# Recurrences stage of a two-block sequence model: rows of the next head issued one step earlier, and three memory tiles placed at other points of the TensorE queue

## The chip, the cores and the metric

The kernel runs on one core of one Trainium2 chip. The metric is device time in microseconds (us). The kernel before takes 3651.59 us, the median of three runs that lie between 3649.14 and 3654.63 us.

## The reference, cut to what matters

The program computes two blocks one after the other for 512 positions of width 1024. The first block projects its input and sends the parts through four sequence mixers, each of four heads. Two of them are decayed attentions in the form that concerns us:

```
# mLSTM, per head: a causal matrix of weights times scores, then a weighted sum of v and of ones
scores = (q . k) / 8 * exp(min(row[t] + col[s], 0)) * causal(s <= t)
num, den = scores @ v, sum(scores)
# SSD (Mamba-2), per head: the same with scores shared by all heads and another row and column
y = ((c . b) * exp(min(row[t] + col[s], 0)) * causal) @ x + d_skip * x
y = rms_norm(y * silu(z)) * gain
```

The second block attends in each of its two layers to a memory of 256 rows. Its keys and values depend on inputs alone: `mkv = mem @ w_mem_kv`, 8 tiles of 128 columns in each layer, 16 tiles in all. They can be computed anywhere ahead of the second block, and the kernel computes them in the stage called recurrences, between the matmuls of the mixers.

## The kernel before, in words

Each stage of the program is a block with one instruction list for each engine. An engine executes its list in order; semaphores carry the dependences; at the end of a stage all engines meet at a barrier (`stage`, line 165). The whole stage that concerns us is the function `recurrences` (line 593), with the class `MemoryTiles` (line 519) for the memory.

The scores of a head are laid out with the source position s on partitions. So a head is four steps j = 0..3: in step j the 128 source positions of block j meet all target positions from block j on, which makes tiles of 128 partitions by 512, 384, 256 and 128 elements. The four heads make 16 steps n = 4h + j, the list `steps`. The mLSTM loop comes first, then the SSD loop; names with `m_` and `s_` tell them apart. A step goes through these engines:

- TensorE: `m_rows(h)` (line 728, matmul L733), once a head, spreads the row of the head over all 128 partitions into PSUM bank 6. It waits until the last exponent of the head before has been read from that bank. In the SSD loop this is `s_rows(h)` (line 755, matmul L760).
- VectorE: `m_exponents(n)` (L1010), or `s_exponents(n)` (L1029), adds the column and clips at zero. The exponents of step n + 1 are in VectorE's list ahead of the weights of step n.
- ScalarE: `m_exps(n)` (L894), `s_exps(n)` (L899): the exponential.
- TensorE, mLSTM alone: `m_score(n)` (L742), q against k, in banks 4 and 5 by turns. The SSD scores were made before and lie in SBUF as `same`.
- VectorE: the causal mask on the diagonal block (L1016, L1035), then the product of scores and decay (L1021, L1041), in double buffers `matt` and `satt`.
- TensorE: `m_sums(n)` (L752 for the values, L753 for the ones, each 64 columns wide), `s_sums(n)` (L766).

TensorE's list in the mLSTM loop is, for each n: `m_score(n + 1)`; if n is the last step of a head, `m_rows` of the next head; `m_sums(n)`; then smaller things that belong to the norms of the other mixers. In the SSD loop it is: if n is the last step of a head, `s_rows` of the next; `s_sums(n)`; matmuls of the norms; and half a memory tile.

A memory tile t takes 24 matmuls of 256 columns. Its weights come from HBM (`sync_load`), ScalarE makes their high part (`scalar_high`, L572), VectorE the low part (`vector_low`, L590), TensorE multiplies (`tensor`, L555, L556 and L561, 12 matmuls in the first half and 4 + 8 in the second), ScalarE copies the result out of PSUM (`scalar_take`, L578), and SyncE stores it (`sync_store`, L540). Two buffers of each kind go round. The first matmul of a tile waits until the result of the tile before has been copied out. Tile 7 stands in the mLSTM loop behind the sums of steps 2 and 3, tiles 8 to 15 in the SSD loop, half a tile behind each of the 16 steps. Tile 15 is the last.

Two of the buffers for the low parts are `kv_low0` and `kv_low1`. The second lies under the first two tiles of `y`, where the SSD output `ys` goes. So VectorE waits, before it writes `ys` (L1184), until all 16 tiles have been multiplied (line 1182).

Behind the SSD loop comes the norm of the SSD output, one step at a time: VectorE adds the skip term (L1184, two instructions) and gates (L1186); ScalarE squares (L981); TensorE sums over the channels (L675); ScalarE takes the root (L984), in front of which it loads a table; VectorE inverts (L1188); TensorE spreads the inverse (L874); VectorE scales (L1192). With this the stage ends, once the stores have landed too (`sync_end`, line 542).

Of the kernel before, what the change touches and what calls it, by code (L numbers as in the profile page):

```python
# [14 lines left out]
P = 128  # L15
# [577 lines left out]
def recurrences(K, U, gate_up, g, bonus, y, memory):  # L593
# [9 lines left out]
    with ExitStack() as ctx:  # L603
# [8 lines left out]
        vt = K.sb(ctx, "vt", [P, NT, 256])  # L612
        kt = K.sb(ctx, "kt", [P, NT, P])
        b = K.sb(ctx, "b", [P, S])
        e = K.sb(ctx, "e", [P, 2, S])
        qd = K.sb(ctx, "qd", [P, S])
        ki = K.sb(ctx, "ki", [P, S])
# [20 lines left out]
                 "m_abs", "em_spread", "m_max", "m_timed", "m_gated", "m_mean", "m_centred", "m_squared", "m_var", "m_root", "m_inverse", "m_spread",  # L638
                 "s_row", "s_exponent", "s_decayed", "s_masked", "s_weighted", "s_summed",
                 "s_gated", "s_squared", "s_var", "s_root", "s_inverse", "s_spread"]  # L640
        kv_bank = lambda t: B[:, (1 if t < MEM_TILES or t == 9 or t == 11 else 2 if t in (13, 15) else 7), 0:MEM]
        with stage(nc, *names, *MEMORY_SEMS) as (block, *sems):
            memory.signals(sems[len(names):])
            (own, a_own, picked, logit, r_mean, turned, v_taken, a_ready, g_abs, g_exp, g_log, rows_ready,
# [25 lines left out]
            def _(pe):  # L670
# [140 lines left out]
                for n in range(LAST):  # L811
                    if n + 1 < LAST:
                        m_score(n + 1)
                    if n % NT == NT - 1 and n + 1 < LAST:
                        m_rows(n // NT + 1)
                    if n == 2 * NT:
                        pe.wait_ge(memory.taken, MEM_TILES)
                    m_sums(n)
                    if n in (2, 3):
                        memory.tensor(pe, MEM_TILES - 1, n % 2, kv_bank(MEM_TILES - 1))  # L820
                    if n == 1:
                        for t in range(2):
                            pe.wait_ge(l_squared, t + 1)
                            mm = quarter_sums(B[:, 7, t * P:(t + 1) * P], heads, t, True, True)
                        mm.then_inc(l_var, 1)
                    if n == 5:
                        pe.wait_ge(l_inverse, 1)
                        head_spread(B[:, 7, :], 0).then_inc(l_spread, 1)
                    if n == 8:
                        pe.wait_ge(l_scaled, 1)  # L830
                        head_spread(B[:, 7, :], 1).then_inc(l_spread, 1)
# [5 lines left out]
                    mm = nc.tensor.matmul(B[o, h // 2, :], K.c("pick", H, h)[:, 0:64], rows[:, 4, :], start=True, stop=True)  # L837
                mm.then_inc(em_spread, 1)
                for n in range(LAST):
                    if n % NT == NT - 1 and n + 1 < LAST:  # L840
                        s_rows(n // NT + 1)
                    s_sums(n)
                    if n in (5, 6):
                        t = n - 5
                        pe.wait_ge(m_gated, t + 1)
                        nc.tensor.matmul(B[:, 2 + t, :], K.c("mean64"), ym[:, t, :], start=True, stop=True).then_inc(m_mean, 1)
                    if n == 9:
                        for t in range(2):
                            pe.wait_ge(m_squared, t + 1)
                            mm = quarter_sums(B[:, 0, t * P:(t + 1) * P], heads, t, True, True)  # L850
                        mm.then_inc(m_var, 1)
                    t = MEM_TILES + n // 2
                    if n == 0:
                        pe.wait_ge(l_scaled, 2)
                    if n == 2:
                        pe.wait_ge(m_max, 1)
                    if n == 10:
                        pe.wait_ge(m_centred, 2)
                    memory.tensor(pe, t, n % 2, kv_bank(t))
                    if n == 12:  # L860
                        pe.wait_ge(m_inverse, 1)
                        head_spread(B[:, 1, :], 0).then_inc(m_spread, 1)
                        head_spread(B[:, 0, :], 1).then_inc(m_spread, 1)
                pe.wait_ge(s_exponent, LAST)
                for t in range(2):
                    pe.wait_ge(s_squared, t + 1)
                    mm = quarter_sums(B[:, 6, 0:P], K.c("mean256")[:, 0:32], t, t == 0, t == 1)
                mm.then_inc(s_var, 1)
                pe.wait_ge(s_inverse, 1)
                pe.wait_ge(l_scaled, 2)  # L870
                pe.wait_ge(memory.taken, memory.count)
                for c in range(NT):
                    row = K.c("ident")[:, 32 * c:32 * c + 1].to_broadcast([P, P])
                    mm = nc.tensor.matmul(B[:, 7, L[c]], row, root[:, 0, :], start=True, stop=True)  # L874
# [3 lines left out]
            def _(act):  # L878
# [68 lines left out]
                    nc.scalar.activation(sq[:, t, :], yl[:, t, :], ACT.Square).then_inc(l_squared, 1)  # L947
                for n in range(LAST):
                    m_exps(n)
                    if n == 5:  # L950
                        memory.scalar_take(act, MEM_TILES - 1, kv_bank(MEM_TILES - 1))
                        memory.scalar_high(act, MEM_TILES + 1)
                    if n == 3:
                        act.wait_ge(l_var, 1)
                        act.wait_ge(r_scaled, 2)
                        nc.scalar.activation(root[:, :, :], B[:, 7, 0:2 * P].rearrange("p (a b) -> p a b", a=2), ACT.Sqrt,
                                             bias=K.c("eps", P, 0, 1)).then_inc(l_root, 1)
                act.wait_ge(m_summed, LAST)
                nc.scalar.activation(dn[:, :, :], B[:, 0:2, :], ACT.Abs).then_inc(m_abs, 1)
                for n in range(LAST):  # L960
                    s_exps(n)
                    if n >= 3 and n % 2:
                        t = MEM_TILES + (n - 3) // 2
                        memory.scalar_take(act, t, kv_bank(t))
                        if t + 2 < memory.count:
                            memory.scalar_high(act, t + 2)
                    if n == 8:
                        for t in range(2):
                            act.wait_ge(m_centred, t + 1)
                            act.wait_ge(l_var, 1)  # L970
                            nc.scalar.activation(sq[:, t, :], ym[:, t, :], ACT.Square).then_inc(m_squared, 1)
                    if n == 10:
                        act.wait_ge(m_var, 1)
                        act.wait_ge(l_scaled, 2)
                        nc.scalar.activation(root[:, :, :], B[:, 0, 0:2 * P].rearrange("p (a b) -> p a b", a=2), ACT.Sqrt,
                                             bias=K.c("eps", P, 0, 1)).then_inc(m_root, 1)
                memory.scalar_take(act, memory.count - 1, kv_bank(memory.count - 1))
                act.wait_ge(s_gated, 1)
                act.wait_ge(m_var, 1)
                for t in range(2):  # L980
                    nc.scalar.activation(sq[:, t, :], ys[:, t, :], ACT.Square).then_inc(s_squared, 1)  # L981
                act.wait_ge(s_var, 1)
                act.wait_ge(m_spread, 2)
                nc.scalar.activation(root[:, 0, :], B[:, 6, 0:P], ACT.Sqrt, bias=K.c("eps", P, 0, 1)).then_inc(s_root, 1)  # L984

            @block.vector
            def _(dve):
# [191 lines left out]
                        step.go(nc.vector.scalar_tensor_tensor(ym[:, t, :], ym[:, t, :], K.col("mlstm_norm_g", t), B[:, bank, :],  # L1179
                                                               ALU.mult, ALU.mult))  # L1180
                dve.wait_ge(s_summed, LAST)
                dve.wait_ge(memory.product, memory.count)
                for t in range(2):
                    step.go(nc.vector.scalar_tensor_tensor(ys[:, t, :], xc[:, t, :], K.col("ssd_d", t), B[:, 4 + t, :], ALU.mult, ALU.add))  # L1184
                step.all()
# [1556 lines left out]
def first_block(K, a, x, outer):  # L2742

    nc = K.nc
    with ExitStack() as ctx:
        gates = K.sb(ctx, "gates", [P, NT, EXPERTS])
        c1 = ctx.enter_context(ExitStack())
        with ExitStack() as held:
            kv_low1 = K.sb(held, "kv_low1", [P, D], F32R)
        y = K.sb(c1, "y", [P, DT, S])  # L2750
        with ExitStack() as c2:
            with ExitStack() as held:
                K.sb(held, "kept_tiles", [P, R_, S])
                kv_raw0 = K.sb(held, "kv_raw0", [P, D])
                kv_high0 = K.sb(held, "kv_high0", [P, D], F32R)
                kv_low0 = K.sb(held, "kv_low0", [P, D], F32R)
                kv_raw1 = K.sb(held, "kv_raw1", [P, D])
                kv_high1 = K.sb(held, "kv_high1", [P, D], F32R)
                kv_out = K.sb(held, "kv_out", [P, 2, MEM])
            U = K.sb(c2, "U", [P, U_TILES, S])  # L2760
            K.first = K.sb(c2, "first", [P, FIRST_W])
            gate_up = K.sb(c2, "gate_up", [P, P])
            lora = K.sb(c2, "lora", [P, 256])
            g = K.sb(c2, "g", [P, 2, S])
            bonus = K.sb(c2, "bonus", [P, 2, S])
            opening(K, a, x, y, U, lora, gate_up, g, bonus)
            memory = MemoryTiles(K, a, y[:, 4:8, :].rearrange("p t (a m) -> p (t a) m", m=MEM), [kv_raw0, kv_raw1], [kv_high0, kv_high1],
                                 [kv_low0, kv_low1], kv_out)
            recurrences(K, U, gate_up, g, bonus, y, memory)
        with lasting(nc, "kept") as (kept,):  # L2770
            arrival(K, a, x, y, gates, kept, lambda t: K.col("ln1_g", t), lambda t: K.col("ln1_b", t))
            K.mu = K.ps(outer, "x_mu", [P, S])
            mixture(K, a, x, gates, kept, lambda t: K.col("ln2_g", t), lambda t: K.col("ln2_b", t))
        c1.close()
# [1404 lines left out]
```

## Time and profile before

| | |
|---|---|
| three runs, median | 3651.59 us (3649.14 to 3654.63) |
| profiled execution | 3646.04 us, its span 3644.1 us |
| mean granted clock of TensorE | 0.959 of full speed |
| recurrences, from the first mLSTM row to the last scaling | about 390.3 to 518.4 us of the span |

The span is the time from the first instruction to the last in one profiled execution. Times in the trace count from the start of this span. PE is TensorE's matmuls, PEld its weight loads, DVE VectorE, ACT ScalarE, SP SyncE. The granted clock of TensorE is given as a share: 1.00 is 2.4 GHz, 0.50 is 1.2 GHz.

### The profile page before, as it was taken

The page shows a single profiled execution, that of the slowest core. Times are in us where ns is not written, and L with a number is a line of the kernel's source. Part 1 is how long each engine was busy: PE and PEld are TensorE (multiplying, and loading weights), DVE is VectorE, ACT ScalarE, POOL GpSimd, SP SyncE. Part 2 cuts the span into 40 slices and gives each one's busy share as a digit, 9 for nine tenths or more (in the row PEclk, how much of TensorE's full clock was granted, in tenths as well). Part 3 has the DMA queues.
Part 4 walks back from the last instruction along what each step waited for, and adds up shares of the span by engine and source line. Part 5 has one row for each costly group of instructions (what it writes and reads, how often), then busy time and mean ns, then how long its engine had stood idle before and what let it go on. Part 6 is the DMA issues. An engine that isn't in the chain of part 4 may idle for free. (4 is left out here: it accounts for less than half of the span.)

```text
span 3644.1 us, 44870 instructions
## 1 busy us (share of the span) xinstructions
PE 3421.1 (94%) x16696; PEld 2724.1 (75%) x16696; DVE 2505.8 (69%) x2841; ACT 1909.5 (52%) x2146; POOL 209.3 (6%) x202
## 2 busy tenths in 40 slices
PE   8998877999999999999989897999999999799998
PEld 7886455888888888888758775678887877578886
DVE  6654455999999999999657757466526776646542
ACT  4223233887778777777545445254316435434422
POOL 0000000111111111211000000000000000000000
PEclk9988888999999999999989998999999999899999
DMA  4111135999999999999511110133322111023331
GB/s 152 41 30 42 46 109 212 352 367 367 365 369 364 371 368 364 367 366 373 189 55 59 58 57 18 48 104 98 101 79 79 55 53 53 22 72 104 97 100 63
DMA packets 118800, 600.24 MB, mean 165 GB/s; under 512 B 20722, under 2 KB 24194, under 8 KB 68130
## 3 DMA queue, kind: packets, MB, share of 16 engines
q1 hardware_dynamic: 105346, 580.93, 43.8%
q0 software_dynamic: 13312, 17.35, 1.9%
q8 instruction: 98, 1.61, 0.2%
q14 instruction: 44, 0.36, 0.0%
HBM read 586.06 MB, written 28.90 MB: 169 GB/s over the span
## 5 line engine op out<-in xcount | busy, mean ns | idle before, releaser
L2326 DVE TENSOR_TENSOR wl<-raw,wh 128x2048 fp32r<-128x2048 f32 x384 | 873.0, 2287 | 55.5 <-ACT wh L2256 55.5
L2256 ACT ACTIVATE wh<-raw 128x2048 fp32r<-128x2048 f32 x384 | 735.7, 1916 | 192.4 <-PE pu L2201 146.7
L2199 PE MATMUL pu<-wh,Xh 128*128 128x512 f32 x1024 | 410.5, 401 | 0.0
L2200 PE MATMUL pu<-wl,Xh 128*128 128x512 f32 x1024 | 400.4, 391 | 0.0
L2201 PE MATMUL pu<-wh,Xl 128*128 128x512 f32 x1024 | 400.2, 391 | 0.0
L4019 ACT ACTIVATE w_high<-w_raw 128x1024 fp32r<-128x1024 f32 (+1 forms) x120 | 137.0, 1145 | 334.5 <-PE acc L3993 172.0
L4052 DVE TENSOR_TENSOR w_low<-w_raw,w_high 128x1024 fp32r<-128x1024 f32 (+1 forms) x120 | 159.6, 1331 | 199.1 <-PE ps L3951 107.6
L3975 PE MATMUL ps<-x_high,w_high 128*128 128x512 f32 x656 | 255.2, 389 | 0.0
L3976 PE MATMUL ps<-x_low,w_high 128*128 128x512 f32 x656 | 255.2, 389 | 0.0
L2199 PEld LDWEIGHTS pu<-wh,Xh 128*128 128x128 f32 x1024 | 193.0, 188 | 45.9 <-issue 8.1
L2201 PEld LDWEIGHTS pu<-wh,Xl 128*128 128x128 f32 x1024 | 192.9, 188 | 42.5
L2956 PE MATMUL acc<-x_high,w_high 128*128 128x512 f32 x528 | 221.0, 419 | 1.5 <-ACT hq L3287 1.5
L2200 PEld LDWEIGHTS pu<-wl,Xh 128*128 128x128 f32 x1024 | 193.1, 189 | 37.3
L2957 PE MATMUL acc<-x_low,w_high 128*128 128x512 f32 x528 | 209.5, 397 | 0.0
L2199 PE MATMUL pd<-wh,hh 128*128 128x512 f32 x512 | 208.5, 407 | 0.2 <-DVE hl L2340 0.2
L2200 PE MATMUL pd<-wl,hh 128*128 128x512 f32 x512 | 200.1, 391 | 0.0
L2201 PE MATMUL pd<-wh,hl 128*128 128x512 f32 x512 | 200.0, 391 | 0.0
L3538 DVE TENSOR_TENSOR w_low<-w_raw,w_high 128x1024 fp32r<-128x1024 f32 (+1 forms) x104 | 118.3, 1141 | 90.4 <-PE acc L2962 64.0
L3951 PE MATMUL ps<-x_high,w_low 128*128 128x512 f32 x704 | 173.2, 389 | 0.0
L3951 PEld LDWEIGHTS ps<-x_high,w_low 128*128 128x128 f32 x704 | 132.1, 188 | 27.5
L3988 PE MATMUL acc<-h_high,w_high 128*128 128x512 f32 x352 | 143.2, 407 | 1.5 <-DVE h_low L4086 1.5
L3975 PEld LDWEIGHTS ps<-x_high,w_high 128*128 128x128 f32 x656 | 123.1, 188 | 25.6
(710 smaller groups left out, 6852.2 us busy)
## 6 DMA issues: line engine op xcount, KB each, us to landing
raw<-in_exp_w SPq DMA_DIRECT2D x384, 1024.0 KB, 7.7
w_raw<-in_w_in SPq DMA_DIRECT2D x100, 512.0 KB, 3.4
w_raw<-in_w_up SPq DMA_DIRECT2D x88, 512.0 KB, 3.8
w_raw<-in_w_down SPq DMA_DIRECT2D x32, 704.0 KB, 4.0
w_raw<-in_w_out SPq DMA_DIRECT2D x32, 384.0 KB, 3.1
kv_raw<-in_w_mem_kv SPq DMA_DIRECT2D x16, 512.0 KB, 3.7
x<-in_x SPq DMA_DIRECT2D x4, 1024.0 KB, 7.4
w_raw<-in_w_out SPq DMA_DIRECT2D x8, 512.0 KB, 4.3
```

The lines of the kernel that those rows point to most:

```text
L2199: nc.tensor.matmul(o, lh[:, k, :], wh[:, m % PARTS, c], start=(m >= 8 and kh == 0 and kk == 0), stop=False)
L2200: nc.tensor.matmul(o, lh[:, k, :], wl[:, m % PARTS, c], start=False, stop=False)
L2201: mm = nc.tensor.matmul(o, ll[:, k, :], wh[:, m % PARTS, c], start=False, stop=end)
L2256: nc.scalar.activation(wh[:, m % PARTS, :], raw[:, m % RAW, :], ACT.Copy).then_inc(w_high, 1)
L2326: nc.vector.tensor_tensor(wl[:, m % PARTS, :], raw[:, m % RAW, :], wh[:, m % PARTS, :], ALU.subtract).then_inc(w_low, 1)
L2956: nc.tensor.matmul(o, wh[:, n % 3, c], high[:, k, :], start=(k == 0), stop=False)
L2957: nc.tensor.matmul(o, wh[:, n % 3, c], low[:, k, :], start=False, stop=False)
L3951: mm = nc.tensor.matmul(o, wl[:, u % 2, c], high[:, k, :], start=False, stop=(k == DT - 1))
L3975: nc.tensor.matmul(o, wh(u)[:, c], high[:, k, :], start=(k == 0), stop=False)
L3976: nc.tensor.matmul(o, wh(u)[:, c], low[:, k, :], start=False, stop=False)
L3988: nc.tensor.matmul(o, wh(u)[:, c], hh[:, f * PART + k, :], start=(f == 0 and k == 0), stop=False)
L4052: nc.vector.tensor_tensor(wl[:, u % 2, 0:width(u)], raw[:, u % 3, 0:width(u)], wh(u), ALU.subtract).then_inc(low_ready, 1)
```

## The change

In TensorE's list, `m_rows` and `s_rows` of the next head stand behind the sums of the head's third step (n % 4 == 2) instead of before the sums of its last step; in the mLSTM loop this puts the row ahead of `m_score` of the next head's first step, in the SSD loop ahead of the half memory tile of that step. Memory tile 7 moves in one piece in front of the sums of mLSTM step 0. Tiles 14 and 15 leave the SSD loop: tile 14 stands behind the loop in one piece, tile 15 behind the sums over squares (L675). On ScalarE the copies out of tiles 7, 14 and 15 move accordingly: behind the exponential of step 1, behind the squares, and behind the last root. The second low buffer lies under `e` instead of under `y`; `e` has been used up by then. With this the wait for all 16 tiles ahead of `ys` falls away. Tile 15 uses PSUM bank 3 instead of bank 2, and the last spread waits for 15 copies instead of 16.

```diff
@@ recurrences
         b = K.sb(ctx, "b", [P, S])
+        with ExitStack() as held:
+            memory.wl.append(K.sb(held, "kv_low1", [P, D], F32R))
         e = K.sb(ctx, "e", [P, 2, S])
@@
-        kv_bank = lambda t: B[:, (1 if t < MEM_TILES or t == 9 or t == 11 else 2 if t in (13, 15) else 7), 0:MEM]
+        kv_bank = lambda t: B[:, (1 if t < MEM_TILES or t == 9 or t == 11 else 2 if t == 13 else 3 if t == 15 else 7), 0:MEM]
@@ tensor, mLSTM loop
                     if n + 1 < LAST:
                         m_score(n + 1)
-                    if n % NT == NT - 1 and n + 1 < LAST:
-                        m_rows(n // NT + 1)
                     if n == 2 * NT:
                         pe.wait_ge(memory.taken, MEM_TILES)
+                    if n == 0:
+                        for half in (0, 1):
+                            memory.tensor(pe, MEM_TILES - 1, half, kv_bank(MEM_TILES - 1))
                     m_sums(n)
-                    if n in (2, 3):
-                        memory.tensor(pe, MEM_TILES - 1, n % 2, kv_bank(MEM_TILES - 1))
+                    if n % NT == NT - 2 and n + 2 < LAST:
+                        m_rows(n // NT + 1)
@@ tensor, SSD loop
-                    if n % NT == NT - 1 and n + 1 < LAST:
+                    s_sums(n)
+                    if n % NT == NT - 2 and n + 2 < LAST:
                         s_rows(n // NT + 1)
-                    s_sums(n)
@@
-                    memory.tensor(pe, t, n % 2, kv_bank(t))
+                    if n < 12:
+                        memory.tensor(pe, t, n % 2, kv_bank(t))
@@ tensor, behind the SSD loop
+                for half in (0, 1):
+                    memory.tensor(pe, memory.count - 2, half, kv_bank(memory.count - 2))
                 pe.wait_ge(s_exponent, LAST)
                 for t in range(2):
                     pe.wait_ge(s_squared, t + 1)
                     mm = quarter_sums(B[:, 6, 0:P], K.c("mean256")[:, 0:32], t, t == 0, t == 1)
                 mm.then_inc(s_var, 1)
+                for half in (0, 1):
+                    memory.tensor(pe, memory.count - 1, half, kv_bank(memory.count - 1))
                 pe.wait_ge(s_inverse, 1)
                 pe.wait_ge(l_scaled, 2)
-                pe.wait_ge(memory.taken, memory.count)
+                pe.wait_ge(memory.taken, memory.count - 1)
@@ scalar
-                    if n == 5:
+                    if n == 1:
                         memory.scalar_take(act, MEM_TILES - 1, kv_bank(MEM_TILES - 1))
                         memory.scalar_high(act, MEM_TILES + 1)
@@
-                    if n >= 3 and n % 2:
+                    if 3 <= n < 15 and n % 2:
@@
-                memory.scalar_take(act, memory.count - 1, kv_bank(memory.count - 1))
                 act.wait_ge(s_gated, 1)
                 act.wait_ge(m_var, 1)
                 for t in range(2):
                     nc.scalar.activation(sq[:, t, :], ys[:, t, :], ACT.Square).then_inc(s_squared, 1)
+                memory.scalar_take(act, memory.count - 2, kv_bank(memory.count - 2))
                 act.wait_ge(s_var, 1)
                 act.wait_ge(m_spread, 2)
                 nc.scalar.activation(root[:, 0, :], B[:, 6, 0:P], ACT.Sqrt, bias=K.c("eps", P, 0, 1)).then_inc(s_root, 1)
+                memory.scalar_take(act, memory.count - 1, kv_bank(memory.count - 1))
@@ vector
                 dve.wait_ge(s_summed, LAST)
-                dve.wait_ge(memory.product, memory.count)
@@ first_block: kv_low1 is no longer made under y, and MemoryTiles gets [kv_low0] alone
```

## Rows read from the trace of the kernel before

**Rows 1.** The page: span, and busy time of each engine with its share.

```profile
span 3644.1 us, 44870 instructions
PE 3421.1 (94%) x16696; PEld 2724.1 (75%) x16696; DVE 2505.8 (69%) x2841; ACT 1909.5 (52%) x2146; POOL 209.3 (6%) x202
```

**Rows 2.** Windows: stretch, length, busy time of each engine, granted clock, DMA.

```profile
core 0: us, PE busy (x) PEld busy (x) DVE busy (x) ACT busy (x) POOL busy (x), PEclk, DMA share, GB/s
390.30:449.40 59.10, 50.18 (x162) 20.82 (x161) 25.82 (x55) 16.50 (x28) 0.00 (x0) 0.83 0.08 23
449.40:508.30 58.90, 53.46 (x277) 35.16 (x276) 40.20 (x66) 20.71 (x36) 0.00 (x0) 0.88 0.19 61
493.50:504.70 11.20, 11.02 (x61) 8.47 (x62) 9.31 (x17) 3.11 (x7) 0.00 (x0) 0.85 0.04 14
```

**Rows 3.** TensorE in order of time: start, length, line, [idle before <- releaser].

```profile
389.24 1.12 PE L561 MATMUL B<-mem_parts,kv_low 128*128 128x256 f32 x8
...
391.95 1.77 PE L742 MATMUL B<-U 64*128 64x512 f32 x4 [0.54 <-ACT same L889]
397.13 1.94 PE L752 MATMUL B<-matt,mv 128*64 128x512 f32 x2 [3.41 <-DVE matt L1021]
...
405.06 0.39 PE L555 MATMUL B<-mem_parts,kv_high 128*128 128x256 f32 x1
...
406.69 1.12 PE L742 MATMUL B<-U 64*128 64x512 f32 x2
...
410.81 0.38 PE L555 MATMUL B<-mem_parts,kv_high 128*128 128x256 f32 x1
...
411.39 1.74 PE L561 MATMUL B<-mem_parts,kv_low 128*128 128x256 f32 x8
```

**Rows 4.** TensorE where the second mLSTM head ends.

```profile
422.88 1.12 PE L742 MATMUL B<-U 64*128 64x512 f32 x2
423.93 1.12 PE L733 MATMUL B<-rows,first 4*128 4x512 f32 x2
426.42 0.43 PE L752 MATMUL B<-matt,mv 128*64 128x128 f32 x2 [1.37 <-DVE matt L1021]
```

**Rows 5.** VectorE at the same place.

```profile
425.09 0.75 DVE L1010 TENSOR_SCALAR mdec<-B,gate_cols 128x512 f32<-128x512 f32 x1 [4.43 <-PE B L733]
```

**Rows 6.** TensorE at the second and ahead of the third turn of SSD heads.

```profile
478.40 1.12 PE L760 MATMUL B<-rows,first 4*128 4x512 f32 x2
480.89 0.43 PE L766 MATMUL B<-satt,xt 128*64 128x128 f32 x2 [1.37 <-DVE satt L1041]
...
489.59 0.36 PE L555 MATMUL B<-mem_parts,kv_high 128*128 128x256 f32 x1 [0.39 <-ACT kv_out L578]
```

**Rows 7.** Windows of one granted clock each.

```profile
394.50:401.40 6.90, 4.27 (x6) 1.25 (x6) 2.78 (x7) 3.84 (x6) 0.00 (x0) 0.51 0.00 0
411.60:418.40 6.80, 6.80 (x15) 2.64 (x14) 3.50 (x7) 1.94 (x4) 0.00 (x0) 0.50 0.31 96
428.70:432.10 3.40, 3.40 (x4) 0.60 (x4) 2.18 (x6) 0.72 (x2) 0.00 (x0) 0.50 0.00 0
449.30:452.50 3.20, 3.09 (x11) 0.76 (x10) 1.80 (x4) 2.07 (x3) 0.00 (x0) 1.00 0.00 0
418.40:428.60 10.20, 8.14 (x30) 3.70 (x31) 4.89 (x10) 1.15 (x2) 0.00 (x0) 1.00 0.01 2
```

**Rows 8.** VectorE behind the SSD loop.

```profile
508.31 1.41 DVE L1184 SCALAR_TENSOR_TENSOR y<-U,cols,B 128x512 f32<-128x512 f32 x2 [3.60 <-PE B L561]
...
516.99 1.41 DVE L1192 SCALAR_TENSOR_TENSOR y<-y,cols,B 128x512 f32<-128x512 f32 x2 [2.17 <-PE B L874]
```

**Rows 9.** ScalarE behind the SSD loop.

```profile
512.18 1.28 ACT L984 ACT_TABLE_LOAD   x1
```

**Rows 10.** TensorE's last spread.

```profile
514.88 2.07 PE L874 MATMUL B<-root,const 128*128 128x128 f32 x8 [2.01 <-DVE root L1188]
```

**Rows 11.** The stores of the memory tiles (L540), from issue to landing.

```profile
DMA to landing us min/median/max: 1.9/2.2/3.8
```

More of the change, by code:

```diff
@@ L2747, in first_block @@
         c1 = ctx.enter_context(ExitStack())
-        with ExitStack() as held:
-            kv_low1 = K.sb(held, "kv_low1", [P, D], F32R)
         y = K.sb(c1, "y", [P, DT, S])
@@ L2767, in first_block @@
             memory = MemoryTiles(K, a, y[:, 4:8, :].rearrange("p t (a m) -> p (t a) m", m=MEM), [kv_raw0, kv_raw1], [kv_high0, kv_high1],
-                                 [kv_low0, kv_low1], kv_out)
+                                 [kv_low0], kv_out)
             recurrences(K, U, gate_up, g, bonus, y, memory)
```

## The prediction

> **What bounds the kernel now.** I read the page first: TensorE is busy 94% of the span [rows 1], so time goes where TensorE waits, or where it works at half clock. The page's chain of waits holds nothing of use here (it follows only the last microseconds), so I went to windows. The two loops take 59.1 and 58.9 us, with TensorE busy 50.2 and 53.5, at a mean clock of 0.83 and 0.88; VectorE is busy 25.8 and 40.2 [rows 2]. So TensorE sets the pace in both, with two losses: gaps, and stretches at half clock.
>
> The gaps are in TensorE's order of time. It idles 3.41 us ahead of the first sums [rows 3] and 1.37 us at a turn of heads [rows 4]. The rows show why: score of the next head (from 422.88), row (from 423.93), and only then can VectorE begin, at 425.09 after 4.43 us of waiting [rows 5]; it makes the next head's exponents first and then the weights that TensorE's next sums need, at 426.42. The same 1.37 us stands at all six turns; one of SSD is shown [rows 6].
>
> The clock: behind several of these gaps TensorE runs at 0.50 for a while [rows 7]. Of 128x512 and smaller matmuls everything then takes twice as long: the eight matmuls of a tile's low part took 1.12 us at full clock and 1.74 us where the clock fell just after their start [rows 3].
>
> **The change, part by part.** Stages meet at barriers, so what the stage loses the program loses.
>
> (a) Tile 7 into the first gap. Before, its first half stands between 405.06 and 406.69 (1.63 us), its second between 410.81 and about 413.05 (the eight low matmuls from 411.39 last 1.74; 2.24 us) [rows 3]. Together 3.9 us leave TensorE's path. At the new place 24 matmuls at 1.12 / 8 = 0.14 us, overlapping to about 0.12, take 2.9 us, and the gap from 393.7 to 397.13 is 3.4 us: hidden. If the clock falls ahead of it the tile takes 5.2 us and 1.8 show. Queued behind it are only `m_sums(0)` and what follows. On ScalarE, its copy and the high part of tile 9 (0.38 + 1.05 us) now stand ahead of the exponential of step 2; VectorE waits there for the score of step 2 anyway, so nothing. Gain 3.9, bounds 2.1 and 3.9.
>
> (b) Three mLSTM rows. The row no longer stands behind the 512-column score, which takes 1.05 us start to start [rows 4]. VectorE gets it 1.05 us earlier, and the score fills 1.05 of the 1.37 us gap. Gain 3 x 1.05 = 3.2; the remaining 0.3 us gap stays. Below: the score now comes 1.1 us later than the row, but VectorE needs it only after 2.9 us of exponents, mask and weights, so no loss.
>
> (c) Three SSD rows. Between row and last sums now lies half a memory tile (12 matmuls, 1.4 us or more), longer than VectorE's 1.37 [rows 6]. So the gap goes whole, 3 x 1.37 = 4.1. At the third turn the row also fills a wait of 0.39 for the copy out of tile 12 [rows 6]. Together 4.5. In the first SSD head VectorE is tied up in two reciprocals and comes free just as the row lands, so its turn could lose 0.5: bounds 3.6 and 4.5.
>
> (d) The end of the SSD loop. Tiles 14 and 15 leave. Before, from the last row's turn (about 493.6) to `ys` (508.31) pass 14.7 us, TensorE-bound. Without the two tiles VectorE sets the pace: 9.31 us busy in 493.5 to 504.7 [rows 2], then the last sums, 0.4 us: 9.8. Its work there (weights, a reciprocal, two low parts, two scalings) is unchanged, and what TensorE keeps (half of tile 13, four sums, two spreads) is 8 us or less even partly at half clock. The wait for all 16 tiles [rows 8] is gone with it. Gain 4.9, bounds 3.5 (if VectorE still waits for a spread) and 5.
>
> (e) The tail. Before: 508.31 to 518.40, 10.1 us [rows 8]. After, counted from the first `ys` instruction: squares end at 3.85 as before (512.18 - 508.31) [rows 8, 9]. Then stands the new wait: the copy out of tile 14 must see its product. The tile starts with `ys`, and takes 2.9 us at full, 5.2 at half clock. Behind this copy (0.38 us) on ScalarE wait the table load (1.28 us) [rows 9], the root, and so VectorE's inverse and the end. At full clock: load 4.2 to 5.5, root 5.9, inverse 6.85. TensorE sums the squares to 4.5, runs tile 15 to 7.35, and only then looks at the inverse: 0.5 us late; spread 1.2 (2.07 at half clock) [rows 10], scaling 1.41: end at 9.95. At half clock throughout: product at 5.2, copy 5.6, inverse 8.25, tile 15 from 6.2 to 11.4, spread 13.5, end 14.9. The last copy and its store (median 2.2 us to landing) [rows 11] end at 7.35 + 0.4 + 0.3 + 2.2 = 10.2, level with VectorE. So the tail changes by between +0.2 less and 4.8 more; TensorE has a gap of about 1.7 us just before, where VectorE sets the pace, so I take part of it at half clock: 1.5 us more.
>
> (f) The clock. In (a) to (e) it is left as it was. At 0.50 TensorE did 4.27 + 6.80 us of work in the first two stretches, and 3.40 in each of three more (from 428.7, 442.3 and 466.2) [rows 7]. Each of the five follows a gap that now shrinks to 0.3 us or nothing. At full clock these 21.3 us would take half: 10.6 less. Off go 0.8 counted in (a), 0.6 for the idle time that the first stretch held, and 0.6 where VectorE then becomes late (the weights of step 8 wait on its scaling): 8.6. Two more stretches I leave out: the one from 493.5 also follows a turn, but lies in (d), where VectorE will set the pace; the one from 452.6 came although TensorE had been busy 3.09 of the 3.20 us before it, with matmuls of four rows [rows 7], and those stay. So a drop without a gap exists. Bounds 0 and 8.6; I take 60%, 5.2.
>
> The Trainium skill ("TensorE: Matmul & The Clock Gate", section "HAM oscillation — how this bites in real kernels") holds that idle gaps cost clock only when much longer than the 1.37 us seen here. The trace disagrees: the clock fell within 3 us behind such a gap at five of the six turns. By the page (f) would be zero, which is rival 1.
>
> Sum: 3.9 + 3.2 + 4.5 + 4.9 - 1.5 + 5.2 = 20.2. Against its own execution: 3646.0 - 20.2 = 3625.8. This execution lies 5.5 us below the median of the three runs; on the scale of the median it is 3651.6 - 20.2 = 3631.4. Edits at nothing: the other PSUM bank (free since the centring of step 7), the other low buffer (`e` was last read before the first memory tile), the weaker wait of the last spread.
>
> **Rivals.**
>
> Rival 1, no clock gain. The gaps close, but half-clock stretches come as often, for another reason than the gaps. For it: the stretch behind 449.3 to 452.5. Against: the mLSTM matmuls from 418.4 to 428.6 ran at 1.00 until a gap had passed [rows 7]. Gain 20.2 - 5.2 = 15.0: 3636.6.
>
> Rival 2, the tail eats it. Both tiles behind the loop run at half clock, the end comes 4.8 us late instead of 1.5, and the clock gain in the loops is absent: (a) to (d) are 16.5, less 4.8 is 11.7, so 3639.9. For it: TensorE was at 0.50 or idle in all of the old tail, the spread took 2.07 [rows 10].
>
> Rival 3, nothing reaches the end: later stages start by the barrier but their own half-clock stretches fall otherwise, by as much as is gained. The runs of before spread by 5.5 us, and this needs three times that. 3651.6.
>
> Rival 4, slower. With tile 7 taken out of the mLSTM loop, and nothing dense left between its short matmuls, TensorE stays at 0.50 from 397 to the end of that loop. Before, this part took 52.3 us (397.1 to 449.4); less 3.9, 3.2 and the 6.9 of (f) that fall in it, it holds 38 us at full clock, so some 75 at half: 23 us lost. Against them stand 4.5 + 4.9 - 1.5 = 7.9 us of (c) to (e): 15 us slower, 3666.7. It decides from 15 us (at full clock) of work more than before that runs at half clock, which is what (a) to (e) bring. Against it: behind 428.7 to 432.1, four sums matmuls and no memory tile, the clock rose again [rows 7].
>
> **How the numbers follow.** Forecast (a clock gain between a third and all) 0.62; rival 1, 0.20; rival 2, 0.07; rival 3, 0.07; rival 4, 0.04. The full clock gain with the best tail gives 25 us and 3626; with runs that differ by 2 or 3 us the low end is 3621. The high end takes in rivals 1 and 2: 3644. A change of under 0.2% (7.3 us) can't be told from none here. Faster: 0.62 + 0.20 + 0.07 less a little for noise, 0.88; same 0.08; slower 0.04.
>
> **What would show it.** (a) The gap ahead of the first sums holds 24 matmuls, and those sums start near 397. (b) TensorE's gaps ahead of L752 at turns are 0.3 us instead of 1.37, and (c) those ahead of L766 vanish. (d) VectorE starts L1184 right behind the last sums, about 9.8 us behind the third turn's. (e) L1184 to the end of L1192 takes 10 to 13 us; the idle time ahead of L874 names the product of tile 15 and not the inverse if the tile is late. (f) The mean clock of the two loops rises from 0.83 and 0.88 to above 0.93. The forecast is wrong if the loops' clock stays, if the tail exceeds 15 us, or if VectorE's idle time ahead of L1010 at turns doesn't fall.

## The result, and the profile after

The changed kernel takes 3632.44 us (median of four runs, 3630.81 to 3633.9) against 3650.36 us for the kernel before beside it (the three runs given with it above and a fourth, of 3645.23): ratio 0.995, 95% interval 0.9935 to 0.9965. It is faster by 17.9 us, clear of the 0.2% that can be told from no change. Forecast were 20.2 us less and 3631.4.

The windows of the changed kernel, cut as in [rows 2]: mLSTM loop, SSD loop up to `ys`, tail; and two stretches at half clock (a granted clock of 0.50).

```profile
span 3628.8 us, 44869 instructions
```

```profile
core 0: us, PE busy (x) PEld busy (x) DVE busy (x) ACT busy (x) POOL busy (x), PEclk, DMA share, GB/s
389.30:436.20 46.90, 44.55 (x162) 20.33 (x161) 25.92 (x55) 16.39 (x28) 0.00 (x0) 0.93 0.09 28
436.20:484.70 48.50, 42.70 (x230) 26.75 (x229) 40.03 (x66) 20.02 (x34) 0.00 (x0) 0.96 0.23 71
484.70:495.30 10.60, 9.12 (x73) 8.56 (x72) 4.99 (x6) 3.57 (x6) 0.00 (x0) 0.84 0.07 25
393.10:396.50 3.40, 3.40 (x18) 3.40 (x17) 1.37 (x3) 2.26 (x3) 0.00 (x0) 0.50 0.06 22
406.70:410.10 3.40, 3.40 (x6) 0.75 (x4) 3.26 (x6) 0.58 (x2) 0.00 (x0) 0.50 0.00 0
```

The span fell from 3644.1 [rows 1] to 3628.8 us. Against [rows 2] the mLSTM loop went from 59.0 to 46.8 us and the SSD loop from 59.0 to 48.6, at a clock of 0.93 and 0.96 instead of 0.83 and 0.88; the tail went from 10.1 to 10.5. TensorE's busy time fell by 5.6 and 10.8 us: the first with the very same matmuls, so that is clock; the second is tiles 14 and 15 gone from the loop, and clock.

TensorE of the changed kernel, in order of time, at the places of [rows 3], [rows 4] and [rows 6]: the tile that now fills the first gap, the turns of two mLSTM heads, and one of SSD.

```profile
395.96 1.35 PE L561 MATMUL B<-mem_parts,kv_low 128*128 128x256 f32 x8
397.23 1.07 PE L754 MATMUL B<-matt,mv 128*64 128x512 f32 x2
...
404.20 1.12 PE L744 MATMUL B<-U 64*128 64x512 f32 x2
405.64 0.43 PE L754 MATMUL B<-matt,mv 128*64 128x128 f32 x2 [0.32 <-DVE matt L1030]
...
415.14 1.12 PE L735 MATMUL B<-rows,first 4*128 4x512 f32 x2
416.19 1.12 PE L744 MATMUL B<-U 64*128 64x512 f32 x2
417.63 0.43 PE L754 MATMUL B<-matt,mv 128*64 128x128 f32 x2 [0.32 <-DVE matt L1030]
...
450.60 0.43 PE L768 MATMUL B<-satt,xt 128*64 128x128 f32 x2 [0.91 <-DVE satt L1050]
...
464.39 0.43 PE L768 MATMUL B<-satt,xt 128*64 128x128 f32 x2
```

The reader is to see the sums at 397.23 without any idle time before them (3.41 us in [rows 3]), the row ahead of the score, 0.32 us instead of 1.37 at a turn, and no idle time at the second SSD turn (464.39). At the first SSD turn (450.60) 0.91 us stay: VectorE is still in its second reciprocal, which ends at 449.4, though the row was there at 448.0.

VectorE in the changed kernel: the first weights, where the second and the third mLSTM head begin, and where the tail begins and ends, against [rows 8]:

```profile
395.31 0.69 DVE L1030 SCALAR_TENSOR_TENSOR matt<-B,mdec 128x512 f32<-128x512 f32 x1
...
404.31 0.75 DVE L1019 TENSOR_SCALAR mdec<-B,gate_cols 128x512 f32<-128x512 f32 x1 [2.87 <-PE B L735]
...
416.30 0.75 DVE L1019 TENSOR_SCALAR mdec<-B,gate_cols 128x512 f32<-128x512 f32 x1 [3.38 <-PE B L735]
...
484.77 1.41 DVE L1192 SCALAR_TENSOR_TENSOR y<-U,cols,B 128x512 f32<-128x512 f32 x2 [0.53 <-PE B L768]
...
491.41 0.95 DVE L1196 RECIPROCAL root<-root 128x128 f32<-128x128 f32 x1 [3.98 <-ACT root L992]
493.86 1.41 DVE L1200 SCALAR_TENSOR_TENSOR y<-y,cols,B 128x512 f32<-128x512 f32 x2 [1.50 <-PE B L882]
```

In the kernel before, VectorE waited 5.55 us for the row where the second head begins, and 4.43 where the third does [rows 5]:

```profile
408.90 0.75 DVE L1010 TENSOR_SCALAR mdec<-B,gate_cols 128x512 f32<-128x512 f32 x1 [5.55 <-PE B L733]
```

These waits are now 2.87 and 3.38 us. The first weights were ready at 396.0 us; the sums that need them began at 397.23, behind tile 7. So the tile, which ran at half clock, did not fit into the gap whole: from the first row to the first sums pass 7.9 us instead of 6.8.

The stage gained 22.3 us between its barriers (200.0 to 177.7), but the span of this execution only 15.3. The opening ahead of it took 0.5 us less, the two stages behind it, whose code is unchanged, 3.1 and 5.3 us more (87.3 to 90.5, 1264.2 to 1269.5), the rest 0.8 less. This difference the experiments had to explain, and what of the stage's gain is place and what is clock.

### The profile page after: what moved, and what is told of

Its sections match the earlier page's. It is cut to its first block and busy times, and to the rows that moved or that the text cites. A ratio compares the mean times of both kernels' runs of the same rounds, so it can differ in the third digit from the quotient of the medians.

```text
span 3628.8 us, 44869 instructions
## 1 busy us (share of the span) xinstructions
PE 3408.8 (94%) x16696; PEld 2718.7 (75%) x16696; DVE 2506.7 (69%) x2841; ACT 1909.2 (53%) x2146; POOL 212.7 (6%) x202
```

## The experiments

All times of loops below run from the first `m_rows` matmul to the first `s_rows` matmul (mLSTM), from there to the first `ys` instruction (SSD), and from there to the end of the last scaling (tail). Ratios are against the kernel before, run on the same chip.

**One part alone.** `rows_only` has both row moves and nothing else, `tile7_only` the moves of tile 7 and its copy, `tail_only` tiles 14 and 15, the low buffer and the waits. Their diffs are parts of the diff above; against the kernel before:

```diff
rows_only, mLSTM loop (the SSD loop alike)
-                    if n % NT == NT - 1 and n + 1 < LAST:
-                        m_rows(n // NT + 1)
...
                     m_sums(n)
+                    if n % NT == NT - 2 and n + 2 < LAST:
+                        m_rows(n // NT + 1)
tile7_only
+                    if n == 0:
+                        for half in (0, 1):
+                            memory.tensor(pe, MEM_TILES - 1, half, kv_bank(MEM_TILES - 1))
                     m_sums(n)
-                    if n in (2, 3):
-                        memory.tensor(pe, MEM_TILES - 1, n % 2, kv_bank(MEM_TILES - 1))
tail_only
-                    memory.tensor(pe, t, n % 2, kv_bank(t))
+                    if n < 12:
+                        memory.tensor(pe, t, n % 2, kv_bank(t))
...
-                dve.wait_ge(memory.product, memory.count)
```

`after_again` is the changed kernel, unchanged.

> The kernel before with only the six rows moved (m_rows and s_rows behind the sums of the third step). The stage recurrences took 200.0 us in the trace of before and 177.7 in that of the changed kernel. By my sum the rows bring 3.2 us (mLSTM) and 4.5 us (SSD), and with the gaps gone most of the half-clock stretches behind the turns: stage near 187 to 189 us, TensorE idle ahead of the last sums of a head 0.3 us (mLSTM) and near 0 (SSD), half-clock time in 390 to 505 us down from 34 us to 20 or less. By the rival (gaps have nothing to do with the clock) the stage takes 192.3 us and the half-clock time stays near 34 us.

> The kernel before with only memory tile 7 moved ahead of the sums of mLSTM step 0, with its copy on ScalarE. By my sum 3.9 us from the tile and about 2 us because the first sums no longer run behind a gap of 3.4 us at half clock: stage near 194 us instead of 200.0. By the rival (no clock effect) 196.1 us. The half-clock stretch from 394.5 should shrink from 6.8 us to 3.4 or nothing.

> The kernel before with only tiles 14 and 15 moved behind the SSD loop, the low buffer under e, and the wait ahead of ys gone. By my sum 4.9 us from the loop's end less 1.5 in the tail: stage near 196.6 us instead of 200.0. By the rival 'the tail eats it' (both tiles at half clock, 4.8 us back) 199.9 us. From the first ys instruction to the end of the last scaling: 10 to 12 us by mine, near 15 by the rival (10.1 before).

> The changed kernel once more, unchanged. In its first trace the stage gained 22.3 us, but the span only 15.3: the next two stages, whose code is the same, took 3.1 and 5.3 us more (87.3 to 90.5 and 1264.2 to 1269.5). If that is scatter from run to run, these stages fall anywhere between 86 and 91, and 1263 and 1270, here and in the other three kernels of this call, whatever their edit; if the change causes it, this kernel shows again both near 90 and 1269.5 and the others lie near before. Recurrences 177 to 180 us in both cases.

Measured, with the half-clock time of each loop in brackets:

```
                     mLSTM        SSD          tail    stage   ratio, 95% interval
before               59.0 (20.5)  59.0 (13.7)  10.1    200.0
rows alone           55.3 (23.9)  53.1 ( 3.4)  10.1    191.9   0.9974 (0.9960 to 0.9987)
tile 7 alone         55.2 (20.5)  58.9 (13.7)  10.1    195.7   0.9995 (0.9984 to 1.0006)
tail alone           58.9 (20.5)  54.4 (13.7)  10.5    195.6   0.9993 (0.9980 to 1.0006)
all (changed)        46.8 ( 6.8)  48.6 ( 3.4)  10.5    177.7   0.9950, again 0.9951
```

In the SSD loop the parts add up: 5.8 and 4.6 us make the 10.4 of the whole. The rows alone lowered its time at half clock from 13.7 to 3.4 us; the tail alone left it at 13.7. In the mLSTM loop the parts don't add up: 3.7 and 3.8 against 12.2. Here neither part alone lowered the time at half clock (20.5 became 23.9 and 20.5), and both together brought it to 6.8, so the missing 4.7 us lie in the clock. How much of them needs both parts together stays open, because the trace of the rows alone began in a state of the clock that most others did not have, as shown below.

The stage with the rows alone, 191.9 us, came out near the 192.3 of the rival and not at 187 to 189. Tile 7 brought 3.8 us, and my 2 us of clock for it did not come: its first stretch at half clock shrank from 6.8 to 3.4 us, but a later one grew by as much. The tail alone neither disproves nor shows a gain in the whole time, but its loop shows 4.6 us.

Two TensorE turns of the kernel with the rows alone, in order of time:

```profile
424.70 0.46 PE L752 MATMUL B<-matt,mv 128*64 128x128 f32 x2 [0.31 <-DVE matt L1021]
...
427.09 1.97 PE L752 MATMUL B<-matt,mv 128*64 128x512 f32 x2
...
438.26 0.43 PE L752 MATMUL B<-matt,mv 128*64 128x128 f32 x2 [0.32 <-DVE matt L1021]
...
440.57 1.97 PE L752 MATMUL B<-matt,mv 128*64 128x512 f32 x2
```

The sums of 512 columns take 1.97 us here and 1.07 above at 397.23: the clock had fallen within half a microsecond of each turn, though the gap was 0.3 us. So a gap of 0.3 us is no protection, and the theory that the gaps cost clock needed a test of its own.

**Close the gaps, leave the rows.** `mrows_fill` is the changed kernel with `m_rows` back at the old place and

```diff
                     if n % NT == NT - 1 and n + 1 < LAST:
                         m_rows(n // NT + 1)
+                        ...
+                        for _ in range(10):
+                            nc.tensor.matmul(B[:, 1 if n < 8 else 7, 0:MEM], memory.wh[0][:, 0:P], memory.high[:, 0, :], start=True, stop=True)
```

> The changed kernel with m_rows back at the old place in the mLSTM loop, and at the three turns, behind m_rows, 10 matmuls of 256 columns on constant operands whose result nobody reads (1.2 us at full clock, for a gap of 1.37). They add work to TensorE and take nothing off the path; they only close the gap. The kernel with tile 7 alone moved has the same mLSTM loop without them: 55.2 us, 20.5 of it at half clock. If the gaps at the turns make the clock fall, the loop falls to about 50 us (46.8 of the changed kernel plus 3 x 1.05) with about 7 us at half clock. If they don't, it stays at 55 us or rises.

The "..." stands for a wait that guards the bank the matmuls write. In the trace TensorE has no idle time ahead of the sums at any of the three turns. The loop took 48.8 us with 3.4 at half clock, 6.4 us less than tile 7 alone, although TensorE was given 30 matmuls more. This speaks for the gaps of 1.37 us as a cost in clock. It is one execution against one, and it can't tell the closed gap from the dense matmuls that closed it.

**Shift the loop in time.** `after_late` and `rows_only_late`, later also `before_late`, have

```diff
+                for _ in range(14):
+                    nc.tensor.matmul(B[:, 0, 0:MEM], memory.high[:, 1, 0:P], memory.high[:, 0, :], start=True, stop=True)
                 m_rows(0)
```

> The changed kernel with 14 matmuls on constant operands (1.7 us) ahead of m_rows(0), result unread. The mLSTM loop behind them is the same, but starts 1.7 us later. Moving the rows alone left this loop with 23.9 us at half clock, the changed kernel twice had 6.8. Theory one: the closed gaps decide; then the loop again takes 46.8 us with about 7 us at half clock. Theory two: where the turns fall in time against the clock's own changes decides, gap or not; then the loop takes 50 us or more, or another number than 46.8 by over 1 us. The stage should take 177.7 + 1.7 = 179.4 us by the first.

> The kernel with the rows alone moved, and the same 14 matmuls (1.7 us) ahead of m_rows(0). There the loop took 55.3 us with 23.9 at half clock, although its gaps at the turns were 0.3 us. By theory two (timing against the clock's own changes) the loop now comes out at another length, between 47 and 55 us. By theory one (the tile between the turns, not the timing, matters) it stays at 55.3 within 0.5 us.

> The kernel before with 14 matmuls on constant operands (1.7 us) ahead of m_rows(0), result unread. With its gaps of 3.4 and 1.37 us it should fall to half clock behind most turns wherever these lie, so the mLSTM loop stays within 2 us of 59.0 by the theory that gaps matter and timing only adds to it; by the theory that timing alone decides it comes out as freely as the changed loop, 50 to 66 us.

The changed loop came out at 44.9 us (3.4 at half clock), the loop with the rows alone at 51.1 (13.7), that of before at 56.9 (17.1): 1.9, 4.2 and 2.1 us less. But more than the start had changed. ScalarE works through its earlier list while the 14 matmuls run, so the wait ahead of the first sums became shorter, here in `before_late`, against 3.41 us in [rows 3]:

```profile
398.98 1.68 PE L752 MATMUL B<-matt,mv 128*64 128x512 f32 x2 [2.35 <-DVE matt L1023]
```

From the first row to the first sums pass 5.2 instead of 6.8 us in the kernel before and in the one with the rows alone, and 5.8 instead of 7.9 in the changed one, where tile 7 now runs at full clock. Behind the first sums the loop of before became 0.5 us shorter, and the changed one did not become shorter at all. Only the loop with the rows alone changed clearly behind its first sums, by 2.6 us. So this experiment shows an effect of timing on the clock at two places, tile 7 and the loop with the rows alone, and decides neither for the theory that the gaps alone matter nor for the theory that timing alone does.

**The same loop by chance.** `better_tail` leaves the mLSTM loop as in the changed kernel and orders the end otherwise: the first half of tile 14 ahead of the sums of step 15, tile 15 ahead of the sums over squares, the copy out of tile 14 ahead of the squares. `better_tail_again` is the same kernel, `before_again` and `after_third` are the kernels before and after, all unchanged.

```diff
+                    if n == 14:
+                        memory.tensor(pe, memory.count - 2, 0, kv_bank(memory.count - 2))
...
-                for half in (0, 1):
-                    memory.tensor(pe, memory.count - 2, half, kv_bank(memory.count - 2))
+                memory.tensor(pe, memory.count - 2, 1, kv_bank(memory.count - 2))
+                for half in (0, 1):
+                    memory.tensor(pe, memory.count - 1, half, kv_bank(memory.count - 1))
                 pe.wait_ge(s_exponent, LAST)
...
-                for half in (0, 1):
-                    memory.tensor(pe, memory.count - 1, half, kv_bank(memory.count - 1))
...
+                memory.scalar_take(act, memory.count - 2, kv_bank(memory.count - 2))
                 act.wait_ge(s_gated, 1)
...
-                memory.scalar_take(act, memory.count - 2, kv_bank(memory.count - 2))
                 act.wait_ge(s_var, 1)
```

> The changed kernel with another order at the end: the first half of tile 14 ahead of the sums of step 15 (TensorE idles 1.68 us there), the second half right behind the loop, tile 15 in front of the sums over squares instead of behind them, and the copy out of tile 14 ahead of the squares. In the changed kernel the table load starts 1.1 us behind the squares, since that copy waits for tile 14, and the last spread waits for tile 15. Both waits should go: from the first ys instruction to the last scaling 9.3 us instead of 10.5, stage 1.2 to 1.5 us shorter (176.3). If the tail is bound by something else (the squares, the table) it stays at 10.5. In the whole time 0.04%, which can't be told from none.

> The kernel with the other order at the end again, beside the changed kernel on one chip. Its tail took 9.9 us instead of 10.5 in the first trace, but its mLSTM loop, which has the same code, 53.9 instead of 46.8. If that was the clock's chance, this loop comes out elsewhere in 45 to 54 and the medians of both kernels lie within 3 us; if the other tail caused it, 53.9 again and the median some 5 us above the changed kernel's.

> The kernel before once more, unchanged. Its mLSTM loop took 59.0 us (20.5 at half clock) in the first trace; the kernels with tile 7 alone and with the tail alone had 20.5 as well. The same mLSTM code as in the changed kernel has meanwhile taken 46.8, 46.8, 44.9 (started 1.7 us later) and 53.9 us (in the kernel with the other tail). If the clock's own changes fall by chance against the program, the loop of before scatters too: 55 to 62 us. If only the changed loop scatters, it is 59.0 again. Also: the two stages behind, 87.3 and 1264.2 us in the first trace, should fall in 87 to 91 and 1264 to 1276, as in the kernels whose code for them is the same.

> The changed kernel a third time, for the interval and one more sample of its mLSTM loop: 45 to 54 us, by how the clock falls; SSD loop to the first ys instruction 48.6 and tail 10.5 as in every trace of it so far, since these repeat to 0.1 us.

```
                     mLSTM        SSD          tail    stage   two stages behind
before, again        58.8 (20.5)  58.9 (13.7)  10.1    199.3    90.2  1268.2
changed, again       46.8 ( 6.8)  48.6 ( 3.4)  10.5    177.7    90.7  1269.8
changed, third       46.8 ( 6.8)  48.6 ( 3.4)  10.5    177.7    87.2  1262.7
better tail          53.9 (23.9)  48.6 ( 3.4)   9.9    185.7    90.4  1265.0
better tail, again   46.8 ( 6.8)  48.6 ( 3.4)   9.9    176.7    88.1  1271.9
```

The mLSTM loop in the first execution of `better_tail`, and its TensorE in order of time at the second turn:

```profile
core 0: us, PE busy (x) PEld busy (x) DVE busy (x) ACT busy (x) POOL busy (x), PEclk, DMA share, GB/s
391.60:445.50 53.90, 52.42 (x161) 22.27 (x160) 25.92 (x55) 16.38 (x28) 0.00 (x0) 0.78 0.08 25
```

```profile
421.85 0.63 PE L755 MATMUL B<-matt,const 128*64 128x128 f32 x2
422.41 1.65 PE L744 MATMUL B<-U 64*128 64x384 f32 x2
423.98 1.97 PE L754 MATMUL B<-matt,mv 128*64 128x512 f32 x2
```

The second execution of the same program:

```profile
386.90:433.70 46.80, 44.46 (x161) 20.27 (x160) 25.89 (x55) 16.39 (x28) 0.00 (x0) 0.93 0.09 29
```

The same instructions take 53.9 or 46.8 us. VectorE and ScalarE have the same busy time in both, TensorE 8.0 us more in the longer one, at a clock of 0.78 instead of 0.93. The two executions differ already ahead of the loop, between the barrier and the first row, where no edit reaches, and in their longest stretch at half clock there:

```profile
319.40:391.58 72.18, 61.22 (x342) 45.97 (x342) 45.71 (x80) 34.16 (x45) 0.00 (x0) 0.83 0.29 92
339.70:356.80 17.10, 15.28 (x62) 11.47 (x62) 11.12 (x23) 11.84 (x15) 0.00 (x0) 0.50 0.20 62
```

against, in the second execution,

```profile
316.70:386.90 70.20, 58.82 (x342) 43.98 (x342) 45.70 (x80) 34.16 (x45) 0.00 (x0) 0.85 0.29 94
336.00:349.70 13.70, 10.96 (x46) 7.97 (x46) 11.47 (x22) 11.99 (x15) 0.00 (x0) 0.50 0.25 78
```

Of the fourteen traces two spent 23.9 us at half clock between barrier and loop and entered the loop 72.2 us behind the barrier: this one, and the one of the rows alone. The other twelve spent 20.5 us there and, without the 14 added matmuls, entered it 70.1 to 70.7 us behind the barrier. The clock first fell 2.7 or 2.8 us behind the loop's start in the two, and not before 3.6 us in the rest. These two are also the two that had 23.9 us at half clock inside the loop. So the 55.3 us of the rows alone carry what this start brings, and can't be set against the 46.8 of the changed kernel to see what the parts are worth together. Why the start differs was not found. The two executions of this program ran on two chips; the other kernels on the chip of the 53.9 us (`mrows_fill`, `after_late`, `rows_only_late`) did not have this start.

The kernel before repeated its own loop, 59.0 and 58.8 us. Taken together, for the mLSTM loop: with tile 7 in the first gap and the later gaps at 0.3 us or nothing it had 3.4 to 6.8 us at half clock in six of seven executions (the changed kernel three times, late, fill, better tail once) and 23.9 in the seventh (better tail); with the rows alone 23.9 and 13.7; with gaps of 1.37 us 17.1 to 20.5 in all five (before twice, late, tile 7, tail).

The SSD loop separates more cleanly. In the nine executions with the SSD rows moved it had 3.4 to 6.8 us at half clock, also where the mLSTM loop ahead of it had 23.9. In the five with the rows at the old place (before twice, late, tile 7, tail) it had 13.7 each time. This shows that moving the rows, which closes the gaps, brings clock; that a small gap does not exclude a fall is shown by the turns above.

The stages behind: over fourteen executions of these kernels, the first took 87.2 to 90.9 us and the second 1262.7 to 1276.1, and the changed kernel had both 87.2 and 90.7, 1262.7 and 1269.8. The 8.4 us that the first pair of traces seemed to lose there are scatter; the first execution of before lay at the low end of both.

The better tail has 9.9 instead of 10.5 us (1.2 were expected, 0.6 came). Its ScalarE:

```profile
498.01 1.28 ACT L993 ACT_TABLE_LOAD   x1
500.01 0.37 ACT L993 ACTIVATE root<-B,const 128x128 f32<-128x128 f32 x1 [0.72 <-PE B L677]
```

The table load no longer waits, but the root does, 0.72 us, for the sums over squares, which now stand behind tile 15. Nor is the 0.6 us a gain of the new order. The changed kernel's 10.5 us hold 3.4 at half clock, the better tail's 9.9 at most 0.4. In `mrows_fill` the tail has the order of the changed kernel and happened to run at full clock, and there it took 9.7:

```profile
489.20:498.90 9.70, 7.82 (x72) 6.99 (x72) 4.98 (x6) 3.46 (x6) 0.00 (x0) 1.00 0.08 27
```

At full clock the other order is therefore no faster (9.9 against 9.7 us). In the whole time it is 0.9945 (0.9932 to 0.9958) beside 0.9946 (0.9933 to 0.9958) for the changed kernel on the same chip: no difference that these runs can tell.

## Why the prediction was right, point by point

- (a) Tile 7: forecast 3.9, measured 3.8 alone. That these agree is in part luck. The tile was not hidden: the clock fell at 393.1, 0.4 us into it, it took 4.5 us instead of 2.9, and it held the first sums up by 1.1 us. I had named that case, with 1.8 us showing. The place alone then brings 3.9 less 1.1, 2.8 us; the other 1.0 came behind the first sums, where the stretches at half clock fell otherwise.
- (b) mLSTM rows: the gap fell from 1.37 to 0.32 at each of three turns, 1.05 each. Right, read off the trace. Alone it can't be timed apart from the clock: 3.7 us with 3.4 more at half clock, and 5.8 in the pair of shifted kernels (56.9 to 51.1) with 3.4 less.
- (c) SSD rows, 4.5: two turns lost their gap whole, the first kept 0.91 us. I had named that (VectorE in its reciprocals, bound 3.6) and chosen the upper end; the lower was right. With the clock this loop gained 5.8 us with the rows alone, and 5.5 in the shifted pair (58.9 to 53.4).
- (d) 4.9 forecast, 4.6 measured alone. VectorE does set the pace there: `ys` starts 9.6 us behind the last turn's sums (475.21 to 484.77), where I had worked out 9.8 and the kernel before took 14.6.
- (e) 1.5 more forecast, 0.4 measured. The waits were the ones named; their size was not. In the changed kernel's ScalarE list:

```profile
487.47 1.15 ACT L988 ACTIVATE sq<-y 128x512 f32<-128x512 f32 x2 [5.86 <-DVE y L1194]
489.31 0.38 ACT L578 ACTIVATE kv_out<-B 128x256 f32<-128x256 f32 x1 [0.70 <-PE B L561]
489.72 1.28 ACT L992 ACT_TABLE_LOAD   x1
```

  The copy out of tile 14 waits 0.70 us, the load starts 1.1 us behind the squares. What I mis-sized is the spread: TensorE was at full clock by then, and it took 1.05 us (492.77 to 493.82) instead of 2.07 [rows 10]. That pays for most of the waits. At full clock throughout I had worked out 9.95 us for the tail; `mrows_fill` measured 9.7.
- (f) 5.2 forecast. The loops show: 12.2 less 3.8 and 3.2 is 5.2 in the mLSTM loop, 10.4 less 4.6 and 3.6 is 2.2 in the SSD loop: 7.4, between my bounds of 0 and 8.6; counting tile 7 at the 2.8 us of its place, it is 8.4. So the clock brought more than I took. And I had taken the 60% as a share of a fixed gain, while the changed loop has more than one outcome: 46.8 or 53.9 us.

The whole was right in its path (gaps closed, and clock gained with them), and near in size partly because misses cancel: the clock brought some 2 to 3 us more than forecast and the tail cost 1.1 less, against 0.9 too much for the SSD rows. The sum of 20.2 stands against 22.2 in the loops and tail, and against 17.9, 17.5 and 18.7 us in the three comparisons of medians. In the profiled executions the changed mLSTM loop was at 46.8 three times of three; that some of the timed ones, which spread from 3620 to 3646 us, met the 53.9 instead would account for the difference, but they have no trace, so this is argued and not shown. The scatter of the stages behind, which is as large, could do it as well.

Rival 1 (no clock gain) is out: the half-clock time of the two loops fell from 34.2 to 10.2 us in the first pair of traces, and in the SSD loop from 13.7 in five executions of five to 3.4 to 6.8 in nine of nine. Filling the mLSTM gaps with useless matmuls shortened that loop by 6.4. With it falls, for this kernel, the advice of the Trainium skill ("TensorE: Matmul & The Clock Gate", "HAM oscillation — how this bites in real kernels") that only far longer gaps cost clock. Rival 2 had the right waits and the wrong clock: 3.4 of the tail's 10.5 us were at half clock, not all. Rival 3 looked true in the first pair of traces (8.4 us lost behind the stage) and was their scatter. Rival 4 is out as a rule: with tile 7 gone from between the turns the loop ran at 0.93. Something like it does happen, in one execution of seven: 23.9 of 53.9 us at half clock.

## What to carry to other kernels

A row or broadcast that the next group's first step needs belongs ahead of work that only the step after it needs: VectorE then starts on it while TensorE does the rest, which was worth 1.05 us a turn in one loop and 0.46 to 1.37 in the other. Independent matmuls are worth most where TensorE waits, and least between two pieces of its own critical work. Where a loop can run at either clock, take several profiles of the same program before any of its microseconds is put down to an edit, and compare the time at half clock in code ahead of the loop that no edit touched; one pair of traces was wrong here by 8 us in stages that had not been touched.

## What the runs showed of the hardware that I had not expected

TensorE's clock made the same matmuls of one loop take 46.8 or 53.9 us, in two executions of one program. The longer one had spent 3.4 us more at half clock (23.9 against 20.5) in unchanged code ahead of the loop, and so had the only other execution with 23.9 us at half clock in this loop. The clock fell at turns with 0.3 us of idle time (at 425.0 and 438.6 in the kernel with the rows alone), and in the changed kernel 0.4 us into a dense tile (393.1), when TensorE had worked without a break for 2.1 us, since 390.97, behind 0.53 us of idle time. What decides in such a case stays open.
